# The first stage of a fused attention and expert-lookup kernel taken out of its loops, and three more rounds of adds moved to VectorE

## The reference, cut to what matters

```
q  = (xb @ w_q)                                  # 8 heads, two halves of 64
s1, s2 = q_half1 . keys1, q_half2 . keys2        # 128 scores each
v1,i1 = top_k(s1,16); v2,i2 = top_k(s2,16)
sc,ci = top_k(v1[:,None]+v2[None,:], 16)         # 16 of 256 sums
e = i1[ci//16]*128 + i2[ci%16];  g = softmax(sc)
a = gelu(u[e] . xb) * g                          # 8*16 = 128 picks for each token
h = h + sum_k a[k] * v[e[k]]
```

## Time and profile before

| | before |
|---|---|
| median of 3 runs | 3063.28 us (3061.88 to 3075.15) |
| the profiled execution | 3063.9 us, span 3062.2 us |
| busy, share of the span | PE 78%, DVE 70%, ACT 40%, POOL 42% |
| traffic | 1176.87 MB, mean 384 GB/s over the span |
| gathers (q0) | 1073.81 MB, 85.8% of 16 DMA engines' span |
| picks, and adds on DVE | 1024, of which 192 |
| first gather issued; first pick taken up by DVE | 138.7 us; 188.3 us |
| mean granted TensorE clock | 0.905 |

### The profile page before, as it was taken

One profiled execution on the slowest core, in us unless ns is written; L12 is line 12 of the kernel. 1 busy time (PEld: TensorE's weight loads), 2 busy tenths in 40 slices (PEclk: granted clock), 3 DMA queues, 4 the chain that ended last, 5 costly groups with the idle time before them and its releaser, 6 DMA issues.

```text
span 3062.2 us, 31998 instructions
## 1 busy us (share of the span) xinstructions
PE 2385.2 (78%) x7648; PEld 1272.7 (42%) x7648; DVE 2157.2 (70%) x4995; ACT 1212.5 (40%) x3525; POOL 1300.3 (42%) x1186
## 2 busy tenths in 40 slices
PE   7548887788877888776986779777887869875677
PEld 6425453354434545242552435333453425422222
DVE  2486578665886658858688775977669686886644
ACT  2123434443433344434444453434534344432333
POOL 0123424444344443434443554344434444345574
PEclk9768999889998999988998989899899989988899
DMA  5469999999999999999999999999999999999998
GB/s 202 154 245 396 405 387 400 412 393 418 384 405 411 396 411 377 403 422 415 408 396 376 411 421 400 359 383 417 413 406 367 370 421 395 396 371 423 422 422 361
DMA packets 164354, 1176.87 MB, mean 384 GB/s; under 512 B 18944, under 2 KB 19200, under 8 KB 22352
## 3 DMA queue, kind: packets, MB, share of 16 engines
q0 software_dynamic: 147456, 1073.81, 85.8%
q1 hardware_dynamic: 16720, 101.03, 8.2%
HBM read 1170.57 MB, written 4.19 MB: 384 GB/s over the span
## 4 chain that ended last, share of the span: by engine, by line
DMA 19%; PE 18%; DVE 12%; issue 8%; POOL 4%; ACT 3%; POOLq 0%; DVEq 0%; ACTq 0%; SPq 0%
DMA ring<-in_uv,pick_now 18%; PE acc L1407 11%; POOL ring L540 4%; DVE ring L901 4%; PE ps L1214 3%; PE ps L1203 1%; DMA xc<-h 1%; PE ps L1342 1%; DVE arena L852 1%; DVE arena L856 1%; DVE arena L844 1%; ACT diag L1136 0%; DVE arena L792 0%; DVE arena L804 0%; PE ps L1212 0%
## 5 line engine op out<-in xcount | busy, mean ns | idle before, releaser
L1407 PE MATMUL acc<-ring,diag 128*128 128x512 f32 x3328 | 1680.1, 653 | 560.9 <-ACT diag L1136 554.5
L540 POOL DMA_INDIRECT ring<-in_uv,pick_now x1024 | 1243.6, 1214 | 1604.7 <-PE acc L1407 1266.7
L901 DVE CUSTOM_DVE_ANT_0 ring<-ring,h_now 128x1024 f32<-128x1024 f32 x1024 | 1232.0, 1222 | 567.0 <-DMA ring<-in_uv,pick_now 555.2
L1407 PEld LDWEIGHTS acc<-ring,diag 128*128 128x128 f32 x3328 | 660.5, 207 | 1483.1 <-ACT diag L1136 790.5
L1123 ACT ACTIVATE gelu<-dots 128x1 f32<-128x1 f32 x1024 | 205.5, 201 | 1243.1 <-DVE dots L901 1193.6
L1136 ACT ACTIVATE diag<-ident,coef 128x128 f32<-128x128 f32 x832 | 334.1, 402 | 87.9 <-PE acc L1407 50.4
L1126 ACT ACTIVATE coef<-gate,gelu 128x1 f32 (+1 forms) x1024 | 301.5, 294 | 110.2
L895 DVE SCALAR_TENSOR_TENSOR side<-ring,coef,side 128x1024 f32<-128x1024 f32 x192 | 246.2, 1283 | 115.5 <-ACT coef L1126 113.5
L1214 PE MATMUL ps<-resident,actT 128*128 128x256 f32 x768 | 179.8, 389 | 0.0
L1214 PEld LDWEIGHTS ps<-resident,actT 128*128 128x128 f32 x768 | 145.8, 193 | 36.0 <-issue 17.5
L1214 PE MATMUL ps<-stream,actT 128*128 128x256 f32 x576 | 136.0, 392 | 16.8 <-ACT actT L976 9.3
(11 more groups left out here) (182 smaller groups left out, 1414.5 us busy)
## 6 DMA issues: line engine op xcount, KB each, us to landing
stream<-in_strips SPq DMA_DIRECT2D x68, 1024.0 KB
resident<-in_strips SPq DMA_DIRECT2D x16, 1024.0 KB, 17.4
ring<-in_uv,pick_now POOLq DMA_INDIRECT x1024
arena<-in_keys SPq DMA_DIRECT2D x8, 512.0 KB
xc<-in_x SPq DMA_DIRECT2D x4, 512.0 KB, 6.4
h<-arena SPq DMA_DIRECT2D x4, 512.0 KB, 10.6
xc<-h SPq DMA_DIRECT2D x4, 512.0 KB, 9.2
out<-arena SPq DMA_DIRECT2D x4, 512.0 KB, 9.8
```

The costliest lines, as they stand in the source:

```text
L540: pool.indirect_dma_start(ring[:, i, :], None, tables[layer], bass.IndirectOffsetOnAxis(ap=pick_now[:, half, i:i + 1], axis=0),).then_inc( ...
L901: dve.tensor_tensor_reduce(ring[:, i, 0:D], ring[:, i, 0:D], h_now[:], 1.0, 0.0, ALU.mult, ALU.add, dots[:, i:i + 1]).then_inc(dotted, 1)
L1407: m = pe.matmul(acc[:, b * 512:(b + 1) * 512], diag[:, i % 4, :], ring[:, i, D + b * 512:D + (b + 1) * 512], start=(r0 == 0 and i == TENSO ...
```

## The change

Two things are changed. First, stage 0 is taken out of the loop on DVE, ACT and PE (POOL and SP keep their loops), and the prep of block 0 ends early: the pieces that `LATE` names, which are parts 1 to 3 of block 0's selection, stand among the first twelve beats of stage 0 instead of ahead of it. The prep of block 1, which then runs in stage 0, has a table of its own, `AT["first"]`, that begins at beat 12 and ends at 63. In this stage DVE adds in rounds 4 to 10. Second, in all other stages DVE adds slots 1, 4 and 7 in rounds 0 to 10 instead of 0 to 7. That is 9 adds more in each of seven stages and 3 fewer in stage 0.

```diff
-VECTOR = ((1, 4, 7),) * 8 + ((),) * 8
-TENSOR = tuple(tuple(i for i in range(SLOTS) if i not in v) for v in VECTOR)
+VECTOR = ((1, 4, 7),) * 11 + ((),) * 5
+VECTOR_FIRST = ((),) * 4 + ((1, 4, 7),) * 7 + ((),) * 5
+TENSOR, TENSOR_FIRST = rest_of(VECTOR), rest_of(VECTOR_FIRST)
...
+    "first": {
+        "pe": {"hT": 15, "q0": 17, "q1": 18, "k0": 20, "k1": 23, "v0": 25, "v1": 26, "v2": 27, "v3": 29, "attn": 30,
...
+        "dve": {"var": 13, "h": 15, "absx": 26, "b": 30, "qd": 31, "mask": 34, "state0": 35, "state1": 37, "o": 37,
+                "x2": 43, "var2": 43, "h2": 43, "pick00": 45, "pick01": 45, "pick02": 45, "pick03": 45, "pick04": 45,
...
+LATE = {
+    "pe": {"sc3": 0},
+    "act": {"ex1": 0, "ev3": 0, "ex2": 2, "ex3": 11},
+    "dve": {"pick10": 0, "pick11": 0, "pick12": 0, "pick13": 0, "pick14": 0, "pick15": 0, "pick16": 0, "pick17": 0,
+            "pick20": 1, "pick21": 1, "pick22": 1, "pick23": 1, "pick24": 2, "pick25": 2, "pick26": 3, "pick27": 7,
+            "pick30": 7, "pick31": 7, "pick32": 8, "pick33": 9, "pick34": 9, "pick35": 11, "pick36": 12,
+            "pick37": 12},
+}
+def opening(engine):
+    return {name: LATE[engine].get(name, name) for name in AT["gla"][engine]}
...
-            for piece in gla(Prep("gla", 0), {name: name for name in AT["gla"]["dve"]}):
+            rest = gla(Prep("gla", 0), opening("dve"))
+            for piece in rest:
...
+                if piece in LATE["dve"].values():
+                    break
-            with dve.Fori(0, BLOCKS - 1) as s:
-                stage(s, Prep("gla", s + 1))
+            stage(0, chain([piece], rest, gla(Prep("gla", 1), AT["first"]["dve"])))
+            with dve.Fori(1, BLOCKS - 1) as s:
+                stage(s, preps(Prep("gla", s + 1)))
```

More of the change, by code:

```diff
@@ L1 @@
 from contextlib import ExitStack
+from itertools import chain
 import numpy as np
@@ L367, in serve @@
                     if beat == 0:
-                        while done + (n + 1) * per <= until and VECTOR[r + n] == VECTOR[r] and (not n or r > 0 and FOLD_AT not in (r, r + n)):
+                        while done + (n + 1) * per <= until and vector[r + n] == vector[r] and (not n or r > 0 and FOLD_AT not in (r, r + n)):
                             n += 1
@@ L1150, in close, with stage @@
                                    ACT.Copy).then_inc(acc_taken, 1)
-            def stage(s, prep):
-                beside(act, passed["act"], serve(s), preps(prep) if prep else ())
+            def stage(s, prep, pieces):
+                beside(act, passed["act"], serve(s), pieces, shares(s)[0])
                 close(s, prep)
@@ L1159, in _ @@
             layer = [0]
-            for piece in gla(Prep("gla", 0), {name: name for name in AT["gla"]["act"]}):
+            rest = gla(Prep("gla", 0), opening("act"))
+            for piece in rest:
                 if piece == "ln":
@@ L1165, in _ @@
                                        ACT.Sin).then_inc(consts_act, 1)
-            with act.Fori(0, BLOCKS - 1) as s:
-                stage(s, Prep("gla", s + 1))
-            stage(BLOCKS - 1, Prep("swa", 0))
+                if piece in LATE["act"].values():
+                    break
+            stage(0, Prep("gla", 1), chain([piece], rest, gla(Prep("gla", 1), AT["first"]["act"])))
+            with act.Fori(1, BLOCKS - 1) as s:
+                stage(s, Prep("gla", s + 1), preps(Prep("gla", s + 1)))
+            stage(BLOCKS - 1, Prep("swa", 0), preps(Prep("swa", 0)))
             layer[0] = 1
             with act.Fori(BLOCKS, STAGES - 1) as s:
-                stage(s, Prep("swa", s - (BLOCKS - 1)))
-            stage(STAGES - 1, None)
+                stage(s, Prep("swa", s - (BLOCKS - 1)), preps(Prep("swa", s - (BLOCKS - 1))))
+            stage(STAGES - 1, None, ())
         @block.tensor
@@ L1413, in fold @@
             def fold(s):
[L1415 to L1416 removed]
+                vector = shares(s)[0]
+                last = max(r for r in range(ROUNDS) if vector[r])
+                pe.wait_ge(used[vector[last][-1]], s * ROUNDS + (last + 2))
                 for b in range(2):
@@ L1420, in fold, with stage @@
                 m.then_inc(side_folded, 1)
-            def stage(s, prep):
+            def stage(s, pieces):
                 pe.wait_ge(acc_taken, s * 2 + 1)
-                beside(pe, passed["pe"], serve(s), preps(prep) if prep else ())
+                beside(pe, passed["pe"], serve(s), pieces, shares(s)[0])
             pe.wait_ge(consts_made, N_CONST_MADE)
             pe.wait_ge(consts_loaded, 16 * N_CONST_LOADS)
[L1429 to L1433, removed]
+            rest = gla(Prep("gla", 0), opening("pe"))
+            for piece in rest:
+                if piece in LATE["pe"].values():
+                    break
+            stage(0, chain([piece], rest, gla(Prep("gla", 1), AT["first"]["pe"])))
+            with pe.Fori(1, BLOCKS - 1) as s:
+                stage(s, preps(Prep("gla", s + 1)))
+            stage(BLOCKS - 1, preps(Prep("swa", 0)))
             with pe.Fori(BLOCKS, STAGES - 1) as s:
-                stage(s, Prep("swa", s - (BLOCKS - 1)))
-            stage(STAGES - 1, None)
+                stage(s, preps(Prep("swa", s - (BLOCKS - 1))))
+            stage(STAGES - 1, ())
 def in_strips(w):
```

37 lines of the change are left out of this document (23 added, 14 removed), and 10 rows, old and new, of the table AT.

## The result

The changed kernel takes 3021.05 us in the median (3016.88 to 3025.1), the kernel before, run beside it, 3062.65. The ratio, taken from the means of four executions of each, is 0.9855, 95% interval 0.9825 to 0.9884, or some 44 us; the medians lie 41.6 us apart, and one execution of the kernel before, at 3075.15, makes the difference. The profiled execution took 3016.88 us, 47 less than the one of the kernel before.

The account below looks back on a forecast made before the run. Transfers were taken to bound the kernel in the steady state, the opening excepted. The terms, -22 + 3 + 3 - 5 = -21 us, took 3063.3 to 3042 us, with a range of 3022 to 3062.

Parts of the forecast that it names:

- Term 1: Opening of stage 0: earlier picks cut idle DMA time from 31.5 to 9.7 us; -22 us, bounds -27 and -15.
- Term 2: Rest of stage 0: block 1's prep squeezed into beats 12 to 63 costs +3 us, bounds 0 and +10.
- Term 3: 60 more adds on DVE: +3 us in stages 1 and 2, -5 us in stages 3 to 6, -2 in all.
- the third bullet: Round 10 of stages 3 to 6: fewer adds relieve PE by 10.6 us, half the lost time returns; -5 us.
- the signs that I had named: Wrong if stage 0's DMA share fell below 0.95, coefficient waits passed 0.6 us, or rounds 10 and 11 grew over 5 us.
- PE's relief is worth all that is lost behind it: Rounds 10 and 11: all time lost behind PE comes back, making the adds worth -19 us; 3025 us, chance 0.13.
- The handed-on gain: Stage 0 becomes bound by block 1's squeezed prep, so the opening's gain shrinks; 3058 us, chance 0.22.
- the slower case: Rounds 8 to 10: adds waiting for coefficients hold up picks on DVE; 3081 us held likeliest, up to 3156, chance 0.13.
- the 77 us by which 60 adds could have held up POOL: If DVE's two-input adds block POOL's descriptor generation, issues slip up to 77 us, hidden by POOL's idle 1604.7 us.

Follow-up runs that it names:

- adds_only: The kernel before with adds on DVE in rounds 0 to 10 of every stage, nothing reordered: ratio 0.9944, 17 us faster.
- adds_narrow: The kernel before with adds on DVE in rounds 0 to 10, those in rounds 8 to 10 covering 8 of 1024 columns: ratio 0.9945.
- adds_8_and_9: The kernel before with adds on DVE in rounds 0 to 9 of every stage, nothing reordered: ratio 0.9947, 16 us faster.

## Why the prediction was right and wrong

**Term 1, the opening: right in its mechanism, a little small.** The schedule held within 2 us: part 1 ended at 155.2 as forecast, the ninth gather left at 162.0, the 25th pick began at 217.5 (217 forecast). What was mis-sized is the lag. I took 6 us from a pick's end to the next gather, and 7 to data flow, throughout, from a row at the lower clock. It was 5.7 us for pick 0 (156.3 to 162.0) and 3.9 for pick 2 (165.6 to 169.5): PE's clock rose with the picks (granted 0.99 from 161 to 195 us, where it had been 0.50). By the windows above the idle DMA time is 1.5 + 3.1 = 4.6 us against 31.5, so 27 us and not 22: the end of the bounds at which I had put a shorter lag. The forecast share of 0.8 from 161 to 195 us was 0.91. What I did not weigh is that this rests on stage 0 having no adds in rounds 0 to 3. With them it is 6 to 9 us less.

**Term 2, the denser rest of stage 0: wrong in sign.** Forecast +3. Of some 33 us that are won up to stage 1 the opening explains 27, which leaves -6 for the rest of the stage; the late table by itself measured -7 (interval -2 to -11). This is the second step that failed, by 9 or 10 us, nearly as much as the third. I had reasoned from averages over the stage (73% and 86% busy) and added a loss to them. The rows of rounds 3 and 11 show that the old table lost transfer time there, which the new one did not. Why this does not carry over to stages 1 and 2 stays open: with the same table the DMA share in round 3 of both was full too, and their length did not change.

**Term 3, the added adds: this is the step that failed.** It had rounds 8 and 9 at nothing ("Nothing there"), because the DMA share in them was 1.01, round 10 of stages 1 and 2 at +3, and round 10 of stages 3 to 6 at -5. The runs give -13 to -17 for the sum, against a forecast of -2, and all of it comes with the adds of rounds 8 and 9. I had read each round's window as if it stood alone. In these rounds PE was full or nearly (18.3 of 18.9 and 20.1 of 20.3 us in the earlier trace rows; 22.8 of 26.1 in round 9 of stage 1) and fell behind, while a ring of eight slots still fed the DMA engines; the debt was paid in rounds 10 and 11, where the share fell: 24 us of idle DMA time over the eight stages, of which adds_only left 7. What I had written in the third bullet, that nine fewer adds take 10.6 us off PE ahead of round 10, was the mechanism; I took half of it for four stages and let DVE's 5.6 us cancel it in two. I had also read too few rows: the DMA share of whole stages runs from 0.96 to 0.99, not 0.97 or 0.98, and round 10 of stages 3 to 6, of which I read stage 4 (0.91), has 0.96, 0.91, 0.94 and 0.91. The short adds show that DVE's part cost nothing there that can be measured. None of the signs that I had named for a wrong forecast would have told: after 217 us the DMA share of stage 0 was 0.98 or more, an add waited 0.53 us for its coefficient on average, and rounds 10 and 11 of stages 1 and 2 together took 54.2 us in each, where they had taken 55.0 and 55.2.

**The rivals.** The one that came in is the second, that PE's relief is worth all that is lost behind it (chance 0.13, 3025), together with an opening better than laid out and term 2 of the other sign. Its -19 for stages 1 to 6 is the idle time that the windows of their rounds 10 and 11 show (19 us); the changed kernel won back some 13 of it. The handed-on gain (term 2 at +10) and the slower case (adds on the path that frees slots) did not: the wait for coefficients is 0.53 us an add, and 76 us of DVE time in adds_narrow weighed nothing. Of the 77 us by which 60 adds could have held up POOL nothing shows: its gathers are busy for 1239.8 us with them, where it was 1243.6.

## What to carry to other kernels

A stretch in which the transfers are saturated can still be where time is lost: look which engine falls behind in it, and price its relief in the stretch that follows, where the buffers have run out. When the consumer of a full ring starts late, take its start out of the queue behind other work, and keep optional work off that engine until the ring turns. A round that gets longer is no loss by itself; set its length against the bytes moved in it. More relief than the backlog needs can cost: four slots were slower than three.

## What the runs showed of the hardware

TensorE's clock answered to relief. Round 9 of stage 1 in the kernel before (the same kind of window):

```profile
756.60:782.70 26.10, 22.78 (x86) 14.46 (x86) 13.20 (x26) 12.10 (x31) 6.82 (x7) 0.93 1.01 421
```

Its mean granted clock is 0.93 there, 0.76 in the changed kernel, with three slots taken off, and 0.67 with four. It does not go by the number of slots alone: adds_only and adds_8_and_9 have three off too, and 0.87 in this round. In the run with four slots it has four matmuls of 128x512 in 1.98 us at the one level (2.4 GHz) and in 3.78 at the other (1.2 GHz), after a pause of 4.9 us. The Trainium skill ("TensorE: Matmul & The Clock Gate", "What's actually happening") has two levels that follow how busy the engine has been; this trace agrees, with those two durations. The round lasted 26.1, 28.8 and 31.3 us, but that is not the clock's price. By length times GB/s it moved 11.0, 12.2 and 12.7 MB; at 421 GB/s the first step, 2.7 us, is transfers alone, and of the second, 2.5 us, about half.
